# FFN gate/up of a hybrid decoder layer: 2x2 block products with seven multiplications on three of eight k-pairs

## The chip, the cores and the metric

One core of a Trainium2 chip runs one launch of the whole layer. The metric is device time in microseconds. TensorE multiplies, VectorE (DVE) and ScalarE (ACT) prepare operands and read results, SyncE (SP) issues the loads of weights; GpSimd (POOL) does next to nothing.

## The reference

The layer has 256 tokens and a width of 2048. All is float32. What the change touches is computed twice, once near the start and once near the end:

```python
def swiglu(h, wg, wu, wd):
    return (jax.nn.silu(h @ wg) * (h @ wu)) @ wd
...
x = x + 0.5 * swiglu(rmsnorm(x, g_ffn1[i]), w1_gate[i], w1_up[i], w1_down[i])
...
x = x + 0.5 * swiglu(rmsnorm(x, g_ffn2[i]), w2_gate[i], w2_up[i], w2_down[i])
```

Gate and up are 2048 x 5632 each, down is 5632 x 2048. Between the two FFNs stand latent attention, dilated window attention, their gates and projections, and after the second a gated embedding term.

## The kernel before

Every product is done in TensorE's fp32r form with operands split in two: a matrix `a` becomes `high = round(a)` and `low = a - high`, and a product is three matmuls, high x high, high x low, low x high. The activations (`hT`, 16 blocks of 128 rows of k by 256 tokens, transposed) are split once. The weights are streamed from HBM in *units* of 512 KB, 128 partitions x 1024 columns of float32, and every unit is split on its way:

- SP loads unit n into `raw[n % 4]` (`square` or `wide`; `SLOTS` = 4) once `lo_ready` says that the unit four before has been split.
- ScalarE copies it to `wh` (L741) once the DMA has landed and TensorE has finished unit n - 4 (`unit_done`).
- VectorE writes `wl = raw - wh` (L1089) and counts `lo_ready` up.
- TensorE waits for `lo_ready`, does 12 matmuls of 512 columns (2 token blocks x 2 halves of the unit x 3), and counts `unit_done` up.

In gate/up a unit is two blocks of k (a *k-pair*) by 512 columns of one matrix. A *turn* is 512 columns of gate and the same 512 of up: 16 units, first the eight k-pairs of gate into PSUM banks 0 and 1, then the eight of up into banks 4 and 5. There are 11 turns in each FFN. In the other engines' programs `ahead(u0 + j, j)` stands once per unit and splits the unit four further on, so that each engine's order is written out by hand: the splits, and between them what else is due.

At a turn's unit 7 ScalarE writes the sigmoid of the scaled gate banks into `sg` (L794) and VectorE multiplies it by the gate (L1134, `gs`); after unit 15 VectorE multiplies by up (L1140). TensorE transposes the eight 128 x 128 blocks of `gs` ahead of unit 2 of the next turn into banks 6 and 7 (`turn_blocks`, L391), and ScalarE and VectorE split them into `aTh` (L813) and `aTl` (L1158). Since the gate banks are read at unit 7 and next written a turn's half later, no unit waits for that.

Down (`down`, written out without a loop on TensorE) multiplies the 44 blocks of `aTh` and `aTl` in two halves of 1024 output columns.

`chain(...)` on VectorE lets an operation count a semaphore and has the next one wait for it: so an operation may read what the one before it wrote.

Of the kernel before, what the change touches and what calls it, by code (L numbers as in the profile page):

```python
# [48 lines left out]
def hybrid_layer(nc, out, x, p, positions, g_ffn1, w1_gate, w1_up, w1_down, g_mix, w_in, g_cq, w_uq,  # L49
# [34 lines left out]
    with ExitStack() as ctx:  # L84
# [138 lines left out]
        def _(sp):  # L223
# [58 lines left out]
            gate_up(U_GU1, w1_gate, w1_up, None)  # L282
            load_tables()
            with sp.Fori(1, FFN_TURNS) as i:
                gate_up(U_GU1, w1_gate, w1_up, i)
# [36 lines left out]
            with sp.Fori(0, FFN_TURNS) as i:  # L322
                gate_up(U_GU2, w2_gate, w2_up, i)
# [1214 lines left out]
```

## Time and profile before

| | us |
|---|---|
| median of 3 runs | 2479.52 (2479.21 to 2479.72) |
| the profiled execution | 2480.78 |
| its span | 2479.0 |
| TensorE busy | 2464.8 |
| VectorE busy | 1347.0 |
| ScalarE busy | 1150.6 |

The span runs from the first to the last instruction of the profile. A busy time is the union of an engine's instructions; matmuls overlap in their pipeline. In groups of instructions the columns are line, engine, operation, output<-input, shapes, count | busy us, mean ns of one | idle before them and what ended it. 450 MB of weights come in over the span.

### The profile page before, as it was taken

How to read it: one execution, taken by the hardware profiler on the slowest of the kernel's cores; microseconds unless marked ns; L12 is line 12 of the kernel's file. 1: busy time of each engine (PE TensorE's matmuls, PEld its weight loads, DVE VectorE, ACT ScalarE, POOL GpSimd, SP SyncE). 2: the span in 40 equal slices, each digit the busy share in tenths (PEclk: the TensorE clock that was granted, in tenths of full speed). 3: DMA queues.
4: the chain of work that ended last, by engine and by line, in shares of the span. 5: the costliest groups of instructions: out<-in, count | busy, mean ns of one | idle time of the engine just before them, and what ended most of it. 6: DMA issues, size and time to landing. Idle time of an engine off the chain costs nothing.

```text
span 2479.0 us, 31100 instructions
## 1 busy us (share of the span) xinstructions
PE 2464.8 (99%) x11314; PEld 2049.4 (83%) x11314; DVE 1347.0 (54%) x1602; ACT 1150.6 (46%) x1383; POOL 0.4 (0%) x5
## 2 busy tenths in 40 slices
PE   8999999999999999999999999999999999999999
PEld 7888888888888887888888888888888888888887
DVE  5555545554546665756655545565555555445455
ACT  5444444443435665455454444454444444434343
POOL 0000000000000000000000000000000000000000
PEclk9999999999999999999999999999999999999999
DMA  7666566655556654666644666656666666666665
GB/s 241 190 187 193 187 187 188 192 189 194 188 187 194 180 161 126 193 182 185 188 119 130 193 195 192 189 179 195 187 191 189 187 192 188 187 194 188 194 191 161
DMA packets 185635, 456.97 MB, mean 184 GB/s; under 512 B 14600, under 2 KB 15824, under 8 KB 185552
## 3 DMA queue, kind: packets, MB, share of 16 engines
q1 hardware_dynamic: 185104, 455.52, 59.9%
q8 instruction: 53, 0.87, 0.1%
q10 hardware_dynamic: 448, 0.34, 0.0%
q14 instruction: 30, 0.25, 0.0%
HBM read 453.70 MB, written 2.10 MB: 184 GB/s over the span
## 4 chain that ended last, share of the span: by engine, by line
PE 99%; DVE 0%; ACT 0%; DMA 0%; issue 0%; ACTq 0%
PE ps L361 45%; PE ps L381 16%; PE ps L383 16%; PE ps L382 16%; PE ps L471 1%; PE ps L391 1%; PE ps L487 1%; PE ps L399 1%; PE ps L498 0%; PE ps L616 0%; DMA res<-in_x 0%; DVE wl L1089 0%; ACT wh L741 0%; DVE vd L1194 0%; PE ps L550 0%; PE ps L552 0%
## 5 line engine op out<-in xcount | busy, mean ns | idle before, releaser
L1089 DVE TENSOR_TENSOR wl<-raw,wh 128x1024 fp32r<-128x1024 f32 x864 | 1056.4, 1225 | 1038.1 <-ACT wh L741 1031.0
L741 ACT ACTIVATE wh<-raw 128x1024 fp32r<-128x1024 f32 x864 | 914.5, 1060 | 1248.7 <-PE ps L383 682.6
L381 PE MATMUL ps<-wh,hT 128*128 128x512 f32 x1664 | 652.2, 392 | 2.2 <-DVE wl L1089 1.5
L383 PE MATMUL ps<-wh,hT 128*128 128x512 f32 x1664 | 648.6, 390 | 0.0
L382 PE MATMUL ps<-wl,hT 128*128 128x512 f32 x1664 | 648.5, 390 | 0.0
L361 PE MATMUL ps<-wh,hT 128*128 128x512 f32 (+1 forms) x1536 | 415.0, 388 | 1.3 <-DVE om L1221 1.1
L381 PEld LDWEIGHTS ps<-wh,hT 128*128 128x128 f32 x1664 | 313.1, 188 | 66.6 <-issue 1.9
L383 PEld LDWEIGHTS ps<-wh,hT 128*128 128x128 f32 x1664 | 312.9, 188 | 65.4
L382 PEld LDWEIGHTS ps<-wl,hT 128*128 128x128 f32 x1664 | 313.2, 188 | 63.8
L361 PEld LDWEIGHTS ps<-wh,hT 128*128 128x128 f32 x1536 | 283.6, 188 | 57.7 <-issue 1.3
L361 PE MATMUL ps<-wl,hT 128*128 128x512 f32 (+1 forms) x768 | 234.5, 387 | 0.0
L361 PE MATMUL ps<-wh,aTh 128*128 128x512 f32 x704 | 217.1, 390 | 0.0
L361 PE MATMUL ps<-wl,aTh 128*128 128x512 f32 x704 | 216.8, 389 | 0.0
L361 PE MATMUL ps<-wh,aTl 128*128 128x512 f32 x704 | 216.7, 389 | 0.0
L361 PEld LDWEIGHTS ps<-wl,hT 128*128 128x128 f32 x768 | 143.0, 188 | 29.1
L361 PEld LDWEIGHTS ps<-wl,aTh 128*128 128x128 f32 x704 | 132.1, 188 | 27.5
L361 PEld LDWEIGHTS ps<-wh,aTl 128*128 128x128 f32 x704 | 132.1, 188 | 27.4
L361 PEld LDWEIGHTS ps<-wh,aTh 128*128 128x128 f32 x704 | 131.8, 188 | 27.1
L361 PE MATMUL ps<-wh,mTh 128*128 128x512 f32 x128 | 39.6, 390 | 0.0
L361 PE MATMUL ps<-wl,mTh 128*128 128x512 f32 x128 | 39.4, 389 | 0.0
L361 PE MATMUL ps<-wh,mTl 128*128 128x512 f32 x128 | 39.4, 389 | 0.0
L1134 DVE SCALAR_TENSOR_TENSOR gs<-ps,small,sg 128x512 f32<-128x512 f32 x44 | 30.9, 743 | 1.7 <-ACT sg L794 1.7
(192 smaller groups left out, 1206.2 us busy)
## 6 DMA issues: line engine op xcount, KB each, us to landing
raw<-in_w_in SPq DMA_DIRECT2D x208, 512.0 KB, 3.6
raw<-in_w_gate SPq DMA_DIRECT2D x176, 512.0 KB, 3.5
raw<-in_w_up SPq DMA_DIRECT2D x176, 512.0 KB, 3.5
raw<-in_w_down SPq DMA_DIRECT2D x176, 512.0 KB, 3.6
raw<-in_w_o SPq DMA_DIRECT2D x32, 512.0 KB, 4.5
raw<-in_w_ple_gate SPq DMA_DIRECT2D x32, 512.0 KB, 3.6
raw<-in_w_br_mla SPq DMA_DIRECT2D x16, 512.0 KB, 4.6
raw<-in_w_br_dil SPq DMA_DIRECT2D x16, 512.0 KB, 3.6
```

The lines of the kernel that those rows point to most:

```text
L361: mm = pe.matmul(ps[:, b0 + 2 * t + m, 0:e - c], a, w[:, s, c:e], start=first, stop=last)
L381: pe.matmul(ps[:, b0 + t, :], xh, wh[:, s, c], start=first, stop=False)
L382: pe.matmul(ps[:, b0 + t, :], xh, wl[:, s, c], start=False, stop=False)
L383: mm = pe.matmul(ps[:, b0 + t, :], xl, wh[:, s, c], start=False, stop=last)
L391: mm = pe.transpose(ps[:, b0 + c // 2, c0:c0 + P], src[:, t, c * P:(c + 1) * P], ident[:, :])
L399: mm = pe.transpose(ps[:, b0 + n, s * S + t * P:s * S + (t + 1) * P], src[:, t, (2 * p + s) * P:(2 * p + s + 1) * P], ident[:, :])
L471: mm = pe.matmul(flat[:, bank * BANK + c:bank * BANK + c + keys], q, k, start=(m == 0), stop=(m == len(parts) - 1))
L487: mm = pe.matmul(ps[:, out_bank + u % 2, 0:P], values(h, t, m), pT[:, m * P:(m + 1) * P], start=(m == 0), stop=(m == n - 1))
L741: act.activation(wh[:, j % SLOTS, :], raw[:, j % SLOTS, :], ACT.Copy).then_inc(hi_ready, 1)
L1089: dve.tensor_tensor(wl[:, j % SLOTS, :], raw[:, j % SLOTS, :], wh[:, j % SLOTS, :].bitcast(F32), ALU.subtract).then_inc(lo_ready, 1)
L1134: dve.scalar_tensor_tensor(out=gs[:, t, :], in0=ps[:, t, :], scalar=inv[:, t:t + 1], in1=sg[:, t, :], op0=ALU.mult, op1=ALU.mult).then_inc ...
```

## The change

In turns 1 to 8 of the 11 of each FFN gate and up are loaded alternately, so that units 2p and 2p+1 are the k-pair p of gate (B11 over B21) and of up (B12 over B22). With the token blocks A11, A21 (first block of k) and A12, A22 (second) that is a product of 2x2 blocks, whose eight block products the k-pairs 1, 3 and 5 replace by seven of sums of blocks. A block product is three matmuls as before.

- The sums of activations (`forms`, split into `FH` and `FL`) are made once per FFN, in turn 0.
- The sums of weights (`sums`, four blocks of 512 columns) are made by VectorE (`sums_of`) once the odd unit has landed; ScalarE rounds them (`TH`), VectorE takes the rest (`TL`). `sums`, `TH` and `TL` exist once. Of the odd unit only the upper half is still split.
- A fast pair is `fast_pair`: two products out of the even unit, one out of the odd, then four with `TH` and `TL` or with a plain block of activations.
- In PSUM a fast turn uses group b0 (four banks, ends that all pairs add to) and group b1 (what the fast pairs share). The groups swap from turn to turn. VectorE combines them: `first_ends` after pair 5, `turn_ends` after unit 15. Silu and the block product then read SBUF (`ends`).
- The transposes move to pair 7. ScalarE only copies the turned blocks out (`aR`, over the place of `aTl`), since `aTh`'s place holds the new buffers; they are split in turns 9, 10 and in down.
- Sigmoid, then gate, then up becomes Silu, then up.
- SP waits for the odd unit of a fast pair before it loads into the slot of the even one.
- The loops of gate/up are written out on all engines. Turns 0, 9 and 10 keep eight products, and turn 9 and 10 wait for the Silu of the turn before at their head.

The core of the diff:

```diff
+        FH, FL = at("FH", 0, [P, 4, 3, P], F32R), at("FL", 6 * KB, [P, 4, 3, P], F32R)
+        sums, ends = at("sums", 12 * KB, [P, 4, BANK]), at("ends", 20 * KB, [P, 4, BANK])
+        TH, TL = at("TH", 28 * KB, [P, 4, BANK], F32R), at("TL", 36 * KB, [P, 4, BANK], F32R)
+        whole_x, forms = at("whole_x", 28 * KB, [P, 3, 2, S]), at("forms", 36 * KB, [P, 4, 3, P])
...
+        FAST_TURNS, FAST_PAIRS = range(1, 9), (1, 3, 5)
...
+        def free_bank(m):
+            return 0 if m % 2 else 4
...
+                        n = m * FFN_BODY + v
+                        p, w = (v // 2, (w_gate, w_up)[v % 2]) if m in FAST_TURNS else (v % 8, (w_gate, w_up)[v // 8])
+                        before = n - SLOTS
+                        square(u0 + n, v, w, 2 * p, m * BANK, 2 if before >= 0 and fast(before) and before % 2 == 0 else 1)
...
-                with pe.Fori(1, FFN_TURNS) as i:
-                    pe.wait_ge(gs_ready, PRIMED + f * T * FFN_TURNS + i * T)
...
-                        square_unit(u0 + i * FFN_BODY + j, j, 2 * j, hTh, hTl, 0, KD)
-                    for j in range(KD // 2):
-                        square_unit(u0 + i * FFN_BODY + KD // 2 + j, j, 2 * j, hTh, hTl, 4, KD)
+                for m in range(1, FFN_TURNS):
+                    if m in FAST_TURNS:
+                        fast_turn(u0, f, m)
+                    else:
+                        plain_turn(u0, f, m)
...
+            def plain_turn(u0, f, m):
+                pe.wait_ge(a_raw, f * FFN_TURNS + m - 1)
+                pe.wait_ge(sig_ready, T * (f * FFN_TURNS + m))
+                for j in range(FFN_BODY):
+                    if j == 4:
+                        pe.wait_ge(am_ready, T * (f * FFN_TURNS + m))
+                        turn_blocks(gs, 6, a_turned)
+                    square_unit(u0 + m * FFN_BODY + j, j, 2 * (j % 8), hTh, hTl, 4 * (j // 8), KD)
...
+            def fast_turn(u0, f, m):
+                u, b0, b1 = u0 + m * FFN_BODY, free_bank(m), free_bank(m + 1)
+                if m == 1:
+                    pe.wait_ge(sig_ready, T * (f * FFN_TURNS + 1))
+                else:
+                    pe.wait_ge(a_raw, f * FFN_TURNS + m - 1)
+                for p in range(KD // 2):
+                    if p == KD // 2 - 1:
+                        pe.wait_ge(am_ready, T * (f * FFN_TURNS + m))
+                        pe.wait_ge(g1_free, f * len(FAST_TURNS) + m)
+                        turn_blocks(gs, b1, a_turned)
+                    if p == FAST_PAIRS[0]:
+                        pe.wait_ge(forms_ready, f + 1)
+                        if m == 1:
+                            pe.wait_ge(am_ready, T * (f * FFN_TURNS + 1))
+                        else:
+                            pe.wait_ge(ends_ready, 2 * (f * len(FAST_TURNS) + m - 1))
+                    if p in FAST_PAIRS:
+                        fast_pair(u + 2 * p, 2 * p, p, FAST_PAIRS.index(p), b0, b1, fasts(f, m, FAST_PAIRS.index(p)))
+                    else:
+                        square_unit(u + 2 * p, 2 * p, 2 * p, hTh, hTl, b0, KD)
+                        square_unit(u + 2 * p + 1, 2 * p + 1, 2 * p, hTh, hTl, b0 + 2, KD)
+            def fast_pair(n, j, p, index, b0, b1, count):
+                s, s1, ka, kb = j % SLOTS, (j + 1) % SLOTS, 2 * p, 2 * p + 1
+                first, last = index == 0, index == len(FAST_PAIRS) - 1
+                def product(bank, x, w, start, stop):
+                    (xh, xl), (yh, yl) = x, w
+                    pe.matmul(ps[:, bank, :], xh, yh, start=start, stop=False)
+                    pe.matmul(ps[:, bank, :], xh, yl, start=False, stop=False)
+                    return pe.matmul(ps[:, bank, :], xl, yh, start=False, stop=stop)
+                def block(k, t):
+                    return hTh[:, k, t * P:(t + 1) * P], hTl[:, k, t * P:(t + 1) * P]
+                def form(a):
+                    return FH[:, a, index, :], FL[:, a, index, :]
+                def weights(slot, c):
+                    return wh[:, slot, c * BANK:(c + 1) * BANK], wl[:, slot, c * BANK:(c + 1) * BANK]
+                def summed(a):
+                    return TH[:, a, :], TL[:, a, :]
+                S1, S3, S2, S4 = (form(a) for a in range(4))
+                T1, T3, T2, T4 = (summed(a) for a in range(4))
+                pe.wait_ge(lo_ready, n + 1)
+                product(b1, block(ka, 0), weights(s, 0), first, last)
+                product(b0, block(kb, 0), weights(s, 1), False, False).then_inc(unit_done, 1)
+                pe.wait_ge(lo_ready, n + 2)
+                product(b0 + 2, S4, weights(s1, 1), False, False).then_inc(unit_done, 1)
+                pe.wait_ge(TL_ready, count + 1)
+                product(b1 + 2, S3, T3, first, last)
+                product(b1 + 3, S1, T1, first, last)
+                product(b1 + 1, S2, T2, first, last)
+                product(b0 + 1, block(kb, 1), T4, False, False).then_inc(fast_done, 1)
...
+                        if half == 0 and k == K - (12 if K == KF else 4):
                             pe.wait_ge(ready, PRIMED + after)
...
+                    target = n + SLOTS
+                    if fast(target) and target % 2:
+                        half_split(u0 + target, target)
+                        sums_high(fasts(f, target // FFN_BODY, FAST_PAIRS.index(target % FFN_BODY // 2)))
+                    else:
+                        ahead(u0 + n, n)
...
+                    if m in FAST_TURNS:
+                        if v == 2 * FAST_PAIRS[-1] + 1:
+                            act.wait_ge(fast_done, fasts(f, m + 1))
+                            act.activation(ends[:, 0, :], ps[:, free_bank(m + 1), :], ACT.Copy).then_inc(p1_out, 1)
+                        if v == FFN_BODY - 3:
+                            turned_out(f, m - 1, free_bank(m + 1))
+                        if v == FFN_BODY - 1:
+                            act.wait_ge(ends_ready, 2 * (f * len(FAST_TURNS) + m) - 1)
+                            silu(f, m, [ends[:, t, :] for t in range(T)])
+                    else:
+                        if v == KD // 2 - 1:
+                            act.wait_ge(unit_done, u0 + n + 1)
...
+                            silu(f, m, [ps[:, t, :] for t in range(T)])
+                        if m and v == 4:
+                            turned_out(f, m - 1, 6)
+                        if m and v in (5, 8, 11, 14):
+                            chunk_high(f, 4 * (m - FAST_TURNS[-1] - 1) + v // 3 - 1)
...
+            def sums_high(count):
+                act.wait_ge(sums_ready, count + 1)
+                if count:
+                    act.wait_ge(fast_done, count)
+                act.activation(TH[:, :, :], sums[:, :, :], ACT.Copy).then_inc(TH_ready, 1)
...
+            def silu(f, m, gates):
+                if f + m:
+                    act.wait_ge(am_ready, T * (f * FFN_TURNS + m))
+                for t in range(T):
+                    act.activation(sg[:, t, :], gates[t], ACT.Silu, scale=inv[:, t:t + 1]).then_inc(sig_ready, 1)
...
+            def chunk_high(f, i):
+                act.wait_ge(a_raw, f * FFN_TURNS + i + 1)
+                act.activation(aTh[:, 4 * i:4 * i + 4, :], aR[:, 4 * i:4 * i + 4, :], ACT.Copy).then_inc(ah_ready, 1)
...
+                for n in range(FFN_TURNS * FFN_BODY):
+                    m, v = divmod(n, FFN_BODY)
+                    target = n + SLOTS
+                    if m in FAST_TURNS and v == FFN_BODY - 1:
+                        turn_ends(u0 + n + 1, m)
+                    if fast(target) and target % 2:
+                        half_split(u0 + target, target)
+                        sums_rest(fasts(f, target // FFN_BODY, FAST_PAIRS.index(target % FFN_BODY // 2)))
+                    else:
+                        ahead(u0 + n, n)
+                    if fast(target) and target % 2 == 0:
+                        sums_of(u0 + target + 1, target % SLOTS,
+                                fasts(f, target // FFN_BODY, FAST_PAIRS.index(target % FFN_BODY // 2)))
+                    if v == 0 and m - 1 in FAST_TURNS:
+                        finish_block(f, m - 1, [ends[:, 2 + t, :] for t in range(T)])
+                    if m == 0:
+                        entry(2 * f, v)
+                        if 8 <= v <= 12:
+                            make_forms(f, v - 8)
+                    if m in FAST_TURNS and v == 2 * FAST_PAIRS[-1] + 1:
+                        first_ends(f, m)
+                    if m not in FAST_TURNS:
+                        if v == FFN_BODY - 1:
+                            dve.wait_ge(unit_done, u0 + n + 1)
+                            finish_block(f, m, [ps[:, 4 + t, :] for t in range(T)])
+                        if m and v in (5, 8, 11, 14):
+                            chunk_rest(f, 4 * (m - FAST_TURNS[-1] - 1) + v // 3 - 1)
+            def make_forms(f, step):
...
+                S1, S3, S2, S4 = (forms[:, a, :, :] for a in range(4))
+                if step == 0:
+                    chain(dve.tensor_tensor(whole_x[:, :, :, :], hi, lo, ALU.add))
+                if step == 1:
+                    chain(dve.tensor_tensor(S1, A21, A22, ALU.add))
+                    dve.tensor_tensor(S3, A11, A21, ALU.subtract)
+                if step == 2:
+                    chain(dve.tensor_tensor(S2, S1, A11, ALU.subtract))
+                if step == 3:
+                    dve.tensor_tensor(S4, A12, S2, ALU.subtract).then_inc(forms_raw, 1)
+                if step == 4:
+                    dve.wait_ge(forms_hi, f + 1)
+                    dve.tensor_tensor(FL[:, :, :, :], forms[:, :, :, :], FH[:, :, :, :].bitcast(F32), ALU.subtract)\
+                       .then_inc(forms_ready, 1)
...
+            def sums_of(n, s, count):
+                if count:
+                    dve.wait_ge(TL_ready, count)
+                dve.wait_ge(raw_in[s + 1], 16 * (n // SLOTS + 1))
+                B11_B12 = raw[:, s:s + 2, 0:BANK]
+                B12_B22 = raw[:, s + 1, :].rearrange("p (a c) -> p a c", a=2)
+                chain(dve.tensor_tensor(sums[:, 0:2, :], B12_B22, B11_B12, ALU.subtract))
+                chain(dve.tensor_tensor(sums[:, 2, :], raw[:, s + 1, BANK:UNIT], sums[:, 0, :], ALU.subtract))
+                dve.tensor_tensor(sums[:, 3, :], raw[:, s, BANK:UNIT], sums[:, 2, :], ALU.subtract).then_inc(sums_ready, 1)
+            def sums_rest(count):
+                dve.wait_ge(TH_ready, count + 1)
+                dve.tensor_tensor(TL[:, :, :], sums[:, :, :], TH[:, :, :].bitcast(F32), ALU.subtract).then_inc(TL_ready, 1)
+            def first_ends(f, m):
+                b1 = free_bank(m + 1)
+                dve.wait_ge(p1_out, f * len(FAST_TURNS) + m)
+                chain(dve.tensor_tensor(ends[:, 3, :], ps[:, b1 + 1, :], ends[:, 0, :], ALU.add))
+                both = ends[:, 3, :].unsqueeze(1).to_broadcast([P, 2, BANK])
+                chain(dve.tensor_tensor(ends[:, 1:3, :], ps[:, b1 + 2:b1 + 4, :], both, ALU.add))
+                dve.tensor_tensor(ends[:, 3, :], ps[:, b1 + 3, :], ends[:, 1, :], ALU.add).then_inc(g1_free, 1)
+            def turn_ends(units, m):
+                dve.wait_ge(unit_done, units)
+                b0 = free_bank(m)
+                for a in range(2):
+                    dve.tensor_tensor(ends[:, 2 * a:2 * a + 2, :], ps[:, b0 + 2 * a:b0 + 2 * a + 2, :],
+                                      ends[:, 2 * a:2 * a + 2, :], ALU.add).then_inc(ends_ready, 1)
+            def finish_block(f, m, ups):
+                if f + m:
+                    dve.wait_ge(a_turned, f * FFN_TURNS + m)
+                if m in FAST_TURNS:
+                    dve.wait_ge(ends_ready, 2 * (f * len(FAST_TURNS) + m))
+                for t in range(T):
+                    dve.wait_ge(sig_ready, T * (f * FFN_TURNS + m) + t + 1)
+                    dve.scalar_tensor_tensor(out=gs[:, t, :], in0=ups[t], scalar=inv[:, t:t + 1], in1=sg[:, t, :],
+                                             op0=ALU.mult, op1=ALU.mult).then_inc(am_ready, 1)
```

## Rows read from the trace of the kernel before

**Rows 1.** The page: TensorE's busy time, and the granted clock in 40 slices.
```profile
PE 2464.8 (99%) x11314; PEld 2049.4 (83%) x11314; DVE 1347.0 (54%) x1602; ACT 1150.6 (46%) x1383; POOL 0.4 (0%) x5
...
PEclk9999999999999999999999999999999999999999
```

**Rows 2.** The page's chain of waits, by line.
```profile
PE ps L361 45%; PE ps L381 16%; PE ps L383 16%; PE ps L382 16%; PE ps L471 1%; PE ps L391 1%; PE ps L487 1%; PE ps L399 1%; PE ps L498 0%; PE ps L616 0%; DMA res<-in_x 0%; DVE wl L1089 0%; ACT wh L741 0%; DVE vd L1194 0%; PE ps L550 0%; PE ps L552 0%
```

**Rows 3.** The chain in order of time: start, length, what; in down.
```profile
512.92 127.86 PE ps L361 x564
```

**Rows 4.** Timeline (start, length), ScalarE, the turned blocks of two turns.
```profile
114.22 1.00 ACT L813 ACTIVATE aTh<-ps 128x1024 f32 x1
...
158.63 1.01 ACT L813 ACTIVATE aTh<-ps 128x1024 f32 x1
```

**Rows 5.** Windows of one turn and of down: busy us per engine, clock, DMA.
```profile
108.40:152.80 44.40, 44.40 (x202) 36.85 (x201) 23.39 (x22) 19.05 (x19) 0.00 (x0) 1.00 0.62 189
504.00:890.00 386.00, 386.00 (x1791) 323.42 (x1790) 215.04 (x259) 196.61 (x300) 0.00 (x0) 1.00 0.60 186
```

**Rows 6.** Who waited for whom: us in total, times, longest.
```profile
DVE wl L1089 <- ACT wh L741: 1031.0, 703, 5.2
ACT wh L741 <- PE ps L383: 682.6, 437, 2.6
```

**Rows 7.** Groups of VectorE by form: split, block product, turned blocks, 512 columns.
```profile
L1089 DVE TENSOR_TENSOR wl<-raw,wh 128x1024 fp32r<-128x1024 f32 x864 | 1056.4, 1225 | 1038.1 <-ACT wh L741 1031.0
L1134 DVE SCALAR_TENSOR_TENSOR gs<-ps,small,sg 128x512 f32<-128x512 f32 x44 | 30.9, 743 | 1.7 <-ACT sg L794 1.7
L1158 DVE TENSOR_TENSOR aTl<-ps,aTh 128x1024 f32 x20 | 24.3, 1217 | 0.0
L1491 DVE TENSOR_TENSOR res<-res,sgp 128x512 f32<-128x512 f32 x4 | 2.8, 692 | 0.1
```

**Rows 8.** Timeline, all engines: a unit ends, the next begins, a slot is split.
```profile
112.83 0.39 PE L383 MATMUL ps<-wh,hT 128*128 128x512 f32 x1
113.05 0.39 PE L381 MATMUL ps<-wh,hT 128*128 128x512 f32 x1
113.25 1.06 ACT L741 ACTIVATE wh<-raw 128x1024 fp32r<-128x1024 f32 x1 [2.55 <-PE ps L383]
114.35 1.23 DVE L1089 TENSOR_TENSOR wl<-raw,wh 128x1024 fp32r<-128x1024 f32 x1 [2.38 <-ACT wh L741]
115.49 1.22 DVE L1158 TENSOR_TENSOR aTl<-ps,aTh 128x1024 f32 x1
```

**Rows 9.** Timeline, VectorE at the end: a chained operation, then an unchained one.
```profile
2471.09 0.69 DVE L1489 TENSOR_TENSOR sgp<-sgp,ps 128x512 f32<-128x512 f32 x1 [5.78 <-PE ps L361]
2471.81 0.69 DVE L1491 TENSOR_TENSOR res<-res,sgp 128x512 f32<-128x512 f32 x1
2472.42 0.68 DVE L1489 TENSOR_TENSOR sgp<-sgp,ps 128x512 f32<-128x512 f32 x1
```

**Rows 10.** Groups of ScalarE by form: split, Sigmoid, turned blocks, 512 columns.
```profile
L741 ACT ACTIVATE wh<-raw 128x1024 fp32r<-128x1024 f32 x864 | 914.5, 1060 | 1248.7 <-PE ps L383 682.6 <-PE ps L361 565.0 <-DMA raw<-in_w_gate 0.9
L794 ACT ACTIVATE sg<-ps,small 128x512 f32<-128x512 f32 x44 | 27.6, 676 | 0.0
L813 ACT ACTIVATE aTh<-ps 128x1024 f32 x20 | 20.2, 1008 | 0.0
L1069 ACT ACTIVATE pTh<-ps 128x512 fp32r<-128x512 f32 x1 | 0.6, 577 | 0.0
```

**Rows 11.** Timeline: TensorE waits for VectorE in the attention stretch.
```profile
906.86 1.28 DVE L1194 TENSOR_SCALAR vd<-ps,small 128x1024 f32<-128x1024 f32 x1
...
908.19 0.73 PE L361 MATMUL ps<-wh,hT 128*128 128x512 f32 x2 [0.20 <-DVE vd L1194]
908.76 0.62 PE L361 MATMUL ps<-wl,hT 128*128 128x512 f32 x2
```

**Rows 12.** DMA issues: count, KB each, median us to landing.
```profile
raw<-in_w_gate SPq DMA_DIRECT2D x176, 512.0 KB, 3.5
...
res<-in_x SPq DMA_DIRECT2D x4, 512.0 KB, 6.9
```

More of the change, by code:

```diff
@@ L281, in _ @@
             load_x(1)
[L282 to L285, printed above, removed]
+            gate_up(U_GU1, w1_gate, w1_up, 0)
             with sp.Fori(0, 2) as i:
@@ L449, in down @@
                             last_turn()
-                        if half == 0 and k == K - 4:
+                        if half == 0 and k == K - (12 if K == KF else 4):
                             pe.wait_ge(ready, PRIMED + after)
@@ L516, in _ @@
             gate_up(U_GU1, 0)
-            pe.wait_ge(gs_ready, PRIMED + T * FFN_TURNS)
-            down(U_DOWN1, aTh, aTl, KF, 1, a_ready, FFN_TURNS - 1, FFN_TURNS, lambda: last_a(0))
+            pe.wait_ge(sig_ready, T * FFN_TURNS)
+            down(U_DOWN1, aTh, aTl, KF, 1, a_ready, FFN_TURNS - 3, FFN_TURNS, lambda: last_a(0))
             for k in range(KD):
@@ L688, in _ @@
             gate_up(U_GU2, 1)
-            pe.wait_ge(gs_ready, PRIMED + 2 * T * FFN_TURNS)
-            down(U_DOWN2, aTh, aTl, KF, 3, a_ready, 2 * FFN_TURNS - 1, 2 * FFN_TURNS, lambda: last_a(1))
+            pe.wait_ge(sig_ready, 2 * T * FFN_TURNS)
+            down(U_DOWN2, aTh, aTl, KF, 3, a_ready, 2 * FFN_TURNS - 3, 2 * FFN_TURNS, lambda: last_a(1))
             j = 0
@@ L825, in down @@
                         ahead(u0 + half * K + k, k)
-                        if half == 0 and k == 3:
-                            last_turn()
+                        if half == 0:
+                            last_turn(k)
                         if half == 0 and meanwhile:
@@ L1154, in turned_rest, with chunk_rest, last_a @@
+            def chunk_rest(f, i):
+                dve.wait_ge(ah_ready, f * FFN_TURNS + i + 1)
+                dve.tensor_tensor(aTl[:, 4 * i:4 * i + 4, :], aR[:, 4 * i:4 * i + 4, :],
+                                  aTh[:, 4 * i:4 * i + 4, :].bitcast(F32), ALU.subtract).then_inc(a_ready, 1)
+            def last_a(f, k):
+                if k in (0, 2, 6):
+                    chunk_rest(f, (8, 9, 9, 10)[k // 2])
             def turned_rest(n, i, ready, dst, hi, done):
@@ L1175, in down @@
                         ahead(u0 + half * K + k, k)
-                        if half == 0 and k == 3:
-                            last_turn()
+                        if half == 0:
+                            last_turn(k)
                         if half == 0 and meanwhile:
@@ L1458, in _ @@
             gate_up(U_GU2, 1)
-            down(U_DOWN2, KF, 3, 0.5, lambda: last_a(1))
+            down(U_DOWN2, KF, 3, 0.5, lambda k: last_a(1, k))
             j = 0
```

145 lines of the change are left out of this document (66 added, 79 removed).

## The prediction

> **What bounds the kernel now.** The page's busy times come first: TensorE is busy 99% of 2479.0 us, with the granted clock at its upper level (2.4 GHz) in every slice, and no clock is to be won back [rows 1]. The chain of waits agrees: it is matmuls almost to the end [rows 2]. In order of time it has 564 matmuls in one unbroken run of 127.86 us, so one matmul costs 0.2267 us; the 390 ns of the groups is the length of one in a pipeline, not its spacing [rows 3]. A unit of weights (512 KB, 12 matmuls) is 2.72 us. In gate/up a turn starts 44.41 us after the last, read from one copy of turned blocks to the next [rows 4]; 192 matmuls make 43.53, eight transposes the other 0.88, and nothing is idle. So each matmul removed is worth its full 0.227 us, as long as VectorE and ScalarE still deliver. They have room now: VectorE is busy 23.4 us of 44.4 [rows 5], and mostly waits for ScalarE, which waits for TensorE to free a slot [rows 6].
>
> **Removed.** A fast pair has seven products of three matmuls (21) instead of 24. 3 pairs x 8 turns x 2 FFNs x 3 = 144 matmuls x 0.2267 = **-32.65 us**. A fast turn is ideally 183 matmuls and 8 transposes, 42.37 us, a gain of 2.04. The same bytes are loaded.
>
> **Prices.** VectorE: 1024 columns 1.225 us, 512 columns 0.69, a scaled product of 512 columns 0.74 [rows 7]; the slope is 1.04 ns per column, so 2048 columns are 2.29 (from the nearest rows: two passes of 1024 give 2.28 as spacing and 2.37 as length). Where the next operation waits for nothing it starts 0.085 us before the last one's end (1.14 us after a 1024 pass), where it waits for ScalarE 0.04 us after ScalarE's end; ScalarE starts 0.20 us after the next unit's first matmul [rows 8]. An operation chained to the one before starts 0.03 us after its end: 0.72 us apart for 512 columns, 0.61 unchained [rows 9]. ScalarE: 1024 columns 1.06, 512 from PSUM 0.58 against 1.01 for 1024, so 512 from SBUF 0.63 and 2048 1.92 (two passes bound it at 2.03) [rows 10]. TensorE starts 0.05 us after VectorE's end and loses 0.1 on the first two matmuls [rows 11].
>
> **Added on VectorE, per fast turn.** 13 full splits at 1.14 (14.8), 3 half splits at 0.60 (1.8), 3 times sums (1.26 + 0.72 + 0.69, 8.0), 3 residuals of 2048 columns at 2.21 (6.6), first ends 2.6, turn ends 2.3, the two block products 1.3: 37.4 us of 42.4. That would fit. But the queue is in order, and behind each sums_of it has only a half split to do while ScalarE makes TH (0.04 + 1.92 + 0.04): 1.4 us idle three times, 41.6 in all. And slots set how far it may run ahead. So I follow the queue. Y is when TensorE starts unit 15, the last of a turn; units are loaded into four slots, and unit n+4 is split once unit n is done.
>
> *To the first fast pair of the next turn.* ScalarE copies slot 2 from Y+0.20 to 1.26; VectorE splits from 1.30, sums from 2.44 to 5.10, two turn ends to 7.38, half split, residual from 7.90 to 10.21. Unit 15, for which the turn ends wait, is done by Y+2.92. TensorE, at its own pace, starts pair 1 at Y+8.16 and needs the residual after nine matmuls, at 10.20: late by 0.06 with the 0.05 of handing over. The wait for the turn ends (7.38) doesn't bind.
>
> *To pair 3.* Let t=0 be the start of pair 1. The residual ended at t=2.05. Now come the split of slot 4 (1.14), the block products (1.32), splits 5 and 6 (2.28), sums (2.66, to 9.38), TH to 11.34, residual to **13.69**. TensorE needs it at 4.76 + 5.44 + 2.04 = 12.24, or 12.30 after the first delay: **a stall of 1.44**. What is queued behind the residual, the splits of slots 8 and 9, isn't late: pair 3's own last 12 matmuls cover it.
>
> *To pair 5.* Splits 8, 9, 10, sums, TH and residual take 10.3 against 10.2 of matmuls: 0.1 late, more or less swallowed by the two restarts. After that there are four plain units and pairs 6 and 7: first ends are through 1.1 us before the transposes need bank group b1, and VectorE is idle again at Y. The lateness doesn't grow from turn to turn.
>
> A turn so loses 1.6 to 1.7 of its 2.04. I take 1.65. This holds for turns 2 to 8: 14 x 1.65 = **+23.1**.
>
> *Turn 1* has no ends before it, but the block products of turn 0 stand behind the residual: 9.41, then to 10.73; pair 1 waits for them, 10.78 - 8.16 + 0.1 = 2.7. VectorE then starts the turn level and is not late at pair 3 (residual at 10.8 of 12.24). Two such: **+5.4**.
>
> *Turn 9* (plain) waits at its head for the silu of turn 8, which needs the first turn end: unit 15 done + 0.20, VectorE 1.22, ScalarE 0.04, two silus 0.58 + 0.73 (Sigmoid's 0.68 and 0.05 for SBUF [rows 10]; Silu isn't in the trace, a copy's 0.63 and 1.06 for 1024 columns bound it), 0.1: 2.9. Before, the gate banks had eight units of cover. Two: **+5.8**.
>
> **At nothing.** The forms (two passes of 1536 columns, four of 384, about 5.7 us per FFN) lie in turn 0, where VectorE idles 1.5 us in each of eight units; uncovered they would cost those 5.7. The aTh/aTl splits, now out of SBUF, move to turns 9, 10 and down: 2.1 us beside 2.72 of matmuls; one more copy of 1.0 goes on ScalarE, which then has 23 us of 42 (13 splits 12.6, half splits 1.6, TH 5.5, the rest 3). Silu takes the place of Sigmoid and of its one table load per FFN. Down waits for all blocks at k=32, the last is there by k=8. Unrolled code runs gapless in down [rows 3]; the loops cost nothing either, so no gain. DMAs: a slot's next load after an even fast unit is held until the odd one's half split; both then go out together. SP is past everything else at that time.
>
> Sum: -32.65 + 23.1 + 5.4 + 5.8 = **+1.7** against the profiled execution, 2480.8, which is 1.3 above the median shown. So 2479.5 + 1.7 = **2481**.
>
> **A rule against a row.** Unchained and chained operations of 512 columns are 0.61 and 0.72 us apart [rows 9]. The Trainium skill, VectorE: DVE Perf Modes, section "The DRAIN you can't avoid", has it that the semaphore after an operation costs nothing extra. The trace disagrees by 0.11.
>
> **Rivals.** *(a) VectorE keeps up, faster.* If the stalls before the residuals vanish, -32.65 + 5.4 + 5.8 = -21.5: 2458. Half of them, 2470. For it: 37.4 of 42.4 us busy, and each saving of 0.1 us per step over the ten steps to pair 3 is 1 us. Against: each step has a row.
>
> *(b) Chaining is free.* Each sums_of is 0.22 shorter: the first residual is in time, pair 3 waits 1.05, pair 5 nothing; 0.6 less per turn, 14 x 0.6 + 0.4 = 8.8 off: 2472. This is what the Trainium skill's rule named above would give; rows 9 speak against it.
>
> *(c) The odd slot comes late, slower.* Slots 6 and 7 are both requested when the half split of slot 3 ends, t=-0.2. In my sum they are there by 3.4 and 5.5: 3.5 us for one load, and the other behind it; VectorE wants slot 6 split by 5.57, and ScalarE has that by 4.5. Loads of x that went out beside others took 6.9 [rows 12]. Then slot 7 lands at 7.2, 0.5 after sums_of wants it (6.71), the same at pair 5 (17.4 for 17.0): 0.9 more per turn, 14 x 0.9 = 12.6: 2494. It decides from 6.9 us after release on. For: 1 MB at once; against: DMA is 62% busy [rows 5].
>
> *(d) It doesn't do what it says:* the matmuls stay at 11314 and the waits come on top, 2514.
>
> **Chances.** Forecast (2475 to 2487) 0.40; (a) 0.25; (b) 0.07; (c) 0.24; (d) and the like 0.04. Under about 0.2%, 5 us, this kernel's measurement can't tell a difference. Faster: (a) and half of (b), 0.29. Same: 0.33 of the forecast, the rest of (b), 0.02 of (c): 0.38. Slower: 0.33. Range 2461 to 2499: 0.25 us of stall per turn is 3.5 us, so it holds stalls from 0.2 to 2.9 per turn.
>
> **What would show it.** Matmuls 11170. Turns 2 to 8 at 44.0 us instead of 44.41, each with one TensorE idle of some 1.4 us behind VectorE's 2048-column residual, at pair 3; at pairs 1 and 5 under 0.2. Turn 1 an idle of 2.6 behind the block product, turn 9 one of 2.8 behind the silu. VectorE busy some 88% in fast turns. Wrong would be: VectorE waiting for loads (c), no idle at pair 3 (a), idle before pairs 1 and 5 as long as before 3 (steps priced too low).

## The result, and the profile after

| | before | changed |
|---|---|---|
| median, 7 runs each on the same chips, us | 2479.52 (2478.07 to 2480.11) | 2486.32 (2484.95 to 2489.76) |
| ratio | | 1.0031, 95% interval 1.0021 to 1.0041 |
| profiled execution, its span | 2480.78, 2479.0 | 2484.95, 2483.2 |
| mean granted clock of TensorE in the 7 runs | | 0.997 to 0.999 |

The changed kernel is 0.3% slower, 6.8 us. The forecast was 2481, the range 2461 to 2499. The execution with the profile was the fastest of the seven; its span is 4.2 us above that of before, and not 6.8, for a reason that lies in the first microseconds of both (last section).

The page of the changed kernel, busy times, then the chain of waits by engine and by line, then the groups of the new operations on VectorE and ScalarE:

```profile
PE 2440.8 (98%) x11170; PEld 2018.1 (81%) x11170; DVE 1589.3 (64%) x1842; ACT 1244.3 (50%) x1470; POOL 0.4 (0%) x5
...
PE 86%; DVE 9%; ACT 2%; issue 2%; DMA 1%; SPq 0%; ACTq 0%
PE ps L382 45%; PE ps L402 10%; PE ps L404 10%; PE ps L403 10%; PE ps L502 2%; DVE TL L1329 2%; PE ps L503 2%; PE ps L504 2%; DVE wl L1222 2%; DVE sums L1323 1%; DVE ends L1344 1%; ACT TH L923 1%; PE ps L561 1%; PE ps L412 1%; PE ps L577 1%
...
L923 ACT ACTIVATE TH<-sums 128x2048 fp32r<-128x2048 f32 x48 | 92.1, 1919 | 147.3 <-DVE sums L1325 147.3
...
L1329 DVE TENSOR_TENSOR TL<-sums,TH 128x2048 fp32r<-128x2048 f32 x48 | 109.9, 2290 | 47.0 <-ACT TH L923 47.0
...
L1323 DVE TENSOR_TENSOR sums<-raw 128x1024 f32<-128x1024 f32 x48 | 58.5, 1218 | 0.0
```

11170 matmuls are 144 fewer than in [rows 1]. The two operations of 2048 columns, of which the kernel before had none, take 2.29 and 1.92 us, as the slope had it. Most telling is the chain of waits: in [rows 2] it is matmuls, here 9% of it is VectorE.

One turn in a window (its ends and length, then busy us of PE, PEld, DVE, ACT, POOL, then the granted clock as a share of 2.4 GHz, the DMA share and GB/s). It runs from the first turn end on VectorE to the next one. It answers to [rows 5]:

```profile
148.57:192.63 44.06, 42.97 (x193) 34.95 (x192) 37.20 (x36) 23.50 (x23) 0.00 (x0) 1.00 0.60 191
```

44.06 instead of 44.41. VectorE is busy 37.2 us instead of 23.4. TensorE's matmuls and transposes would fill 42.37, so 1.69 are lost. Where, the timeline of VectorE says (start, length), from the ends of one turn to pair 3 of the next; the last row is TensorE's:

```profile
148.57 2.35 DVE L1344 TENSOR_TENSOR ends<-ps,ends 128x1024 f32<-128x1024 f32 x2
...
150.84 0.68 DVE L1313 TENSOR_TENSOR wl<-raw,wh 128x512 fp32r<-128x512 f32 x1
151.44 2.29 DVE L1329 TENSOR_TENSOR TL<-sums,TH 128x2048 fp32r<-128x2048 f32 x1
153.64 1.22 DVE L1222 TENSOR_TENSOR wl<-raw,wh 128x1024 fp32r<-128x1024 f32 x1
154.78 1.41 DVE L1354 SCALAR_TENSOR_TENSOR gs<-ends,small,sg 128x512 f32<-128x512 f32 x2
156.10 2.35 DVE L1222 TENSOR_TENSOR wl<-raw,wh 128x1024 fp32r<-128x1024 f32 x2
158.37 1.22 DVE L1323 TENSOR_TENSOR sums<-raw 128x1024 f32<-128x1024 f32 x1
159.62 0.69 DVE L1324 TENSOR_TENSOR sums<-raw,sums 128x512 f32<-128x512 f32 x1
160.35 0.69 DVE L1325 TENSOR_TENSOR sums<-raw,sums 128x512 f32<-128x512 f32 x1
160.96 0.69 DVE L1313 TENSOR_TENSOR wl<-raw,wh 128x512 fp32r<-128x512 f32 x1
163.03 2.29 DVE L1329 TENSOR_TENSOR TL<-sums,TH 128x2048 fp32r<-128x2048 f32 x1 [1.38 <-ACT TH L923]
165.38 0.50 PE L502 MATMUL ps<-TH,FH 128*128 128x512 f32 x1 [1.09 <-DVE TL L1329]
```

Read it as a queue without a gap from 148.57 to 161.6: ends, half split, residual, three splits with the block products between them, sums. Then 1.38 us in which VectorE has nothing to do but wait for TH, then the residual, and TensorE starts 0.06 after it. The residuals end 11.59 us apart (153.73 and 165.32); the matmuls between their uses take 10.2. Measured from start to start of the matmuls of this turn, 1.39 of the 1.69 are lost at pair 3 (1.26 before the first matmul with TH, 0.13 over the next ones), 0.23 at pair 1 and 0.07 at pair 5.

Whom TensorE waited for over the whole execution (us in total, times, longest):

```profile
PE ps L502 <- DVE TL L1329: 15.3, 14, 1.1
...
PE ps L402 <- issue: 5.5, 2, 2.7
PE ps L502 <- issue: 5.1, 2, 2.5
PE ps L382 <- issue: 1.9, 2, 0.9
```

Fourteen times pair 3; twice the head of turn 9 (L402); twice pair 1 of turn 1 (L502); and twice the head of down (L382), which the prediction had left out. The times are from a matmul's modelled end, 0.16 us behind where the next would have started. "Issue" is here a wait whose releaser the profile doesn't show. The timeline has the block products of turn 0 end at 64.96 and the silu of turn 8 at 413.40, each just before the matmul that waited:

```profile
61.35 2.29 DVE L1329 TENSOR_TENSOR TL<-sums,TH 128x2048 fp32r<-128x2048 f32 x1 [1.38 <-ACT TH L923]
63.56 1.40 DVE L1354 SCALAR_TENSOR_TENSOR gs<-ps,small,sg 128x512 f32<-128x512 f32 x2
65.06 0.47 PE L502 MATMUL ps<-wh,hT 128*128 128x512 f32 x1 [2.54 <-issue]
...
410.81 2.36 DVE L1344 TENSOR_TENSOR ends<-ps,ends 128x1024 f32<-128x1024 f32 x2 [0.34 <-PE ps L404]
412.07 1.33 ACT L929 ACTIVATE sg<-ends,small 128x512 f32<-128x512 f32 x2
413.51 0.47 PE L402 MATMUL ps<-wh,hT 128*128 128x512 f32 x1 [2.73 <-issue]
```

The granted clock around turn 1 of the second FFN (windows, columns as above; the clock is the third number from the end), then TensorE there:

```profile
1692.00:1694.00 2.00, 0.65 (x3) 0.19 (x2) 2.00 (x2) 1.45 (x2) 0.00 (x0) 1.00 1.01 380
1694.00:1696.00 2.00, 0.81 (x2) 0.74 (x3) 2.00 (x3) 0.00 (x0) 0.00 (x0) 0.79 0.25 97
1696.00:1698.00 2.00, 2.00 (x6) 1.52 (x6) 1.36 (x2) 0.00 (x0) 0.00 (x0) 0.50 0.35 39
1698.00:1700.00 2.00, 2.00 (x9) 1.64 (x8) 0.72 (x1) 1.61 (x2) 0.00 (x0) 0.86 0.98 341
```

```profile
1695.19 0.76 PE L502 MATMUL ps<-wh,hT 128*128 128x512 f32 x1 [2.54 <-issue]
1695.75 0.63 PE L503 MATMUL ps<-wl,hT 128*128 128x512 f32 x1
1696.18 0.63 PE L504 MATMUL ps<-wh,hT 128*128 128x512 f32 x1
1696.61 0.63 PE L502 MATMUL ps<-wh,hT 128*128 128x512 f32 x1
```

After 2.54 us without a matmul the clock is found to have fallen to 1.2 GHz for 3.4 us in all; matmuls then start 0.43 us apart instead of 0.227, and the stretch costs about 1.7 us. The same idle in the first FFN, 2.54 us as well, has no such stretch in this execution.

### The profile page after: what moved, and what is told of

The parts are those of the page before. It is cut to its first block, busy times and chain, and to the rows that moved or that the text cites. A ratio compares the mean times of both kernels' runs of the same rounds, so it can differ in the third digit from the quotient of the medians.

```text
span 2483.2 us, 29387 instructions
## 1 busy us (share of the span) xinstructions
PE 2440.8 (98%) x11170; PEld 2018.1 (81%) x11170; DVE 1589.3 (64%) x1842; ACT 1244.3 (50%) x1470; POOL 0.4 (0%) x5
## 3 DMA queue, kind: packets, MB, share of 16 engines
q8 instruction: 80, 1.31, 0.2%
## 4 chain that ended last, share of the span: by engine, by line
PE 86%; DVE 9%; ACT 2%; issue 2%; DMA 1%; SPq 0%; ACTq 0%
PE ps L382 45%; PE ps L402 10%; PE ps L404 10%; PE ps L403 10%; PE ps L502 2%; DVE TL L1329 2%; PE ps L503 2%; PE ps L504 2%; DVE wl L1222 2%; DVE sums L1323 1%; DVE ends L1344 1%; ACT TH L923 1%; PE ps L561 1%; PE ps L412 1%; PE ps L577 1%
## 5 line engine op out<-in xcount | busy, mean ns | idle before, releaser
L1222 DVE TENSOR_TENSOR wl<-raw,wh 128x1024 fp32r<-128x1024 f32 x816 | 988.3, 1223 | 748.4 <-ACT wh L831 745.8
L831 ACT ACTIVATE wh<-raw 128x1024 fp32r<-128x1024 f32 x816 | 857.7, 1058 | 969.1 <-PE ps L382 564.8
L402 PE MATMUL ps<-wh,hT 128*128 128x512 f32 x1280 | 501.7, 392 | 7.9 <-issue 5.5
L404 PE MATMUL ps<-wh,hT 128*128 128x512 f32 x1280 | 498.3, 389 | 0.0
L403 PE MATMUL ps<-wl,hT 128*128 128x512 f32 x1280 | 498.1, 389 | 0.0
L382 PE MATMUL ps<-wh,hT 128*128 128x512 f32 (+1 forms) x1536 | 415.0, 388 | 1.2 <-DVE om L1431 1.0
L382 PEld LDWEIGHTS ps<-wh,hT 128*128 128x128 f32 x1536 | 283.5, 188 | 57.5 <-issue 1.2
L402 PEld LDWEIGHTS ps<-wh,hT 128*128 128x128 f32 x1280 | 240.4, 188 | 57.6 <-issue 8.2
L404 PEld LDWEIGHTS ps<-wh,hT 128*128 128x128 f32 x1280 | 240.3, 188 | 50.1
L403 PEld LDWEIGHTS ps<-wl,hT 128*128 128x128 f32 x1280 | 240.5, 188 | 48.6
L382 PE MATMUL ps<-wl,hT 128*128 128x512 f32 (+1 forms) x768 | 234.5, 387 | 0.0
L382 PE MATMUL ps<-wh,aTh 128*128 128x512 f32 x704 | 217.3, 390 | 1.9 <-issue 1.9
L382 PE MATMUL ps<-wh,aTl 128*128 128x512 f32 x704 | 216.8, 389 | 0.0
L382 PE MATMUL ps<-wl,aTh 128*128 128x512 f32 x704 | 216.7, 389 | 0.0
L382 PEld LDWEIGHTS ps<-wl,hT 128*128 128x128 f32 x768 | 143.0, 188 | 29.1
L923 ACT ACTIVATE TH<-sums 128x2048 fp32r<-128x2048 f32 x48 | 92.1, 1919 | 147.3 <-DVE sums L1325 147.3
L382 PEld LDWEIGHTS ps<-wh,aTh 128*128 128x128 f32 x704 | 131.7, 188 | 29.7 <-issue 2.6
L382 PEld LDWEIGHTS ps<-wh,aTl 128*128 128x128 f32 x704 | 132.2, 188 | 27.5
L382 PEld LDWEIGHTS ps<-wl,aTh 128*128 128x128 f32 x704 | 132.2, 188 | 27.4
L1329 DVE TENSOR_TENSOR TL<-sums,TH 128x2048 fp32r<-128x2048 f32 x48 | 109.9, 2290 | 47.0 <-ACT TH L923 47.0
L502 PE MATMUL ps<-TH,FH 128*128 128x512 f32 x144 | 60.0, 416 | 15.3 <-DVE TL L1329 15.3
L1323 DVE TENSOR_TENSOR sums<-raw 128x1024 f32<-128x1024 f32 x48 | 58.5, 1218 | 0.0
```

Source lines behind the costliest of these rows:

```text
L382: mm = pe.matmul(ps[:, b0 + 2 * t + m, 0:e - c], a, w[:, s, c:e], start=first, stop=last)
L402: pe.matmul(ps[:, b0 + t, :], xh, wh[:, s, c], start=first, stop=False)
L403: pe.matmul(ps[:, b0 + t, :], xh, wl[:, s, c], start=False, stop=False)
L404: mm = pe.matmul(ps[:, b0 + t, :], xl, wh[:, s, c], start=False, stop=last)
L502: pe.matmul(ps[:, bank, :], xh, yh, start=start, stop=False)
L831: act.activation(wh[:, j % SLOTS, :], raw[:, j % SLOTS, :], ACT.Copy).then_inc(hi_ready, 1)
```

## The experiments

All are made from the changed kernel, but the last. Each was timed beside the kernel before on the same chip. For gap, gap_early, turn0 and heads that kernel took 2479.51 there, as beside the changed kernel (2479.52). For moved, all4 and idle20, on another chip, it took 2477.90: their distance to the changed kernel is therefore taken from their distances to the kernel before, each on its own chip.

**gap.** In turns 2 to 8 the block products fill the wait for TH.

```diff
                         half_split(u0 + target, target)
+                        if v == 3 and m - 1 in FAST_TURNS:
+                            finish_block(f, m - 1, [ends[:, 2 + t, :] for t in range(T)])
                         sums_rest(...)
...
-                    if v == 0 and m - 1 in FAST_TURNS:
+                    if v == 0 and m - 1 == FAST_TURNS[-1]:
```

> The block products of turn m-1 move from behind the split of slot 4 to behind the half split of pair 3, where VectorE idles 1.38 us for TH. Order theory: they leave the leg to pair 3 (1.32 us). But slot 6 is then the limit: ScalarE had it split 4.8 us into pair 1 in the changed kernel, so VectorE splits at 4.8 and not at 4.25, and the stall at pair 3 goes from 1.44 to about 0.6: turns 2 to 8 at 43.3 instead of 44.06, 14 x 0.8 = 11 us faster, 2475. Were only VectorE's steps in the way: stall 0.1, 18 us, 2468. Load theory (slots 6 and 7 decide): VectorE only idles more, stall 1.2 or more, under 3 us faster.

Measured: 2475.32 (2472.93 to 2480.85, 11 runs), ratio to the kernel before 0.9985 [0.9976, 0.9994]: 11.0 us under the changed kernel. VectorE in the same leg:

```profile
156.99 2.35 DVE L1222 TENSOR_TENSOR wl<-raw,wh 128x1024 fp32r<-128x1024 f32 x2
159.57 1.23 DVE L1222 TENSOR_TENSOR wl<-raw,wh 128x1024 fp32r<-128x1024 f32 x1 [0.23 <-ACT wh L831]
...
163.91 1.41 DVE L1356 SCALAR_TENSOR_TENSOR gs<-ends,small,sg 128x512 f32<-128x512 f32 x2
165.38 2.29 DVE L1331 TENSOR_TENSOR TL<-sums,TH 128x2048 fp32r<-128x2048 f32 x1
```

and ScalarE, whose split of slot 6 waited for the load:

```profile
158.47 1.06 ACT L831 ACTIVATE wh<-raw 128x1024 fp32r<-128x1024 f32 x1 [1.39 <-DMA raw<-in_w_gate]
```

The products now stand where nothing else could, and the residual starts the moment TH is there (ScalarE ends it at 165.34). The third split waits for ScalarE and that for the load. The load was not what held the changed kernel, but it is next in line. The turns of the first FFN take 42.87 to 43.47 us, on average 43.13 (43.3 was expected): 14 x 0.94 = 13 us less. The medians show 11.0; the profiled execution has one stretch at the lower clock more than that of the changed kernel.

**gap_early.** The same, and slots 6 and 7 are let go earlier.

```diff
                         half_split(u0 + target, target)
+                        if m in FAST_TURNS and v == FFN_BODY - 1:
+                            turn_ends(u0 + n + 1, m)
...
-                    if m in FAST_TURNS and v == FFN_BODY - 1:
+                    if m == FAST_TURNS[-1] and v == FFN_BODY - 1:
                         turn_ends(u0 + n + 1, m)
...
```

> As gap, and the half split of slot 3 goes ahead of the two turn ends, so that the loads of slots 6 and 7 are let go 2.3 us earlier. Turn ends are then through 0.2 us before pair 1 wants them. Order theory with the load as second limit: stall at pair 3 0.1 to 0.2, turns at 42.8, 14 x 1.25 = 17.5 us faster than the changed kernel, 2469, and 6 us faster than gap. If the load is no limit: the same as gap.

Measured: 2469.32 (2467.76 to 2472.09, 5 runs), 0.9958 [0.9945, 0.9972], 6.0 under gap. VectorE does the three splits in one piece:

```profile
153.72 3.49 DVE L1222 TENSOR_TENSOR wl<-raw,wh 128x1024 fp32r<-128x1024 f32 x3
```

and TensorE's waits for TL are no longer among its own; only its weight loads show them, 0.3 at most:

```profile
PEld ps L502 <- DVE TL L1333: 9.1, 42, 0.3
```

**moved.** The counter-test: the same 1.32 us out of one leg and into the next.

```diff
-                    if v == 0 and m - 1 in FAST_TURNS:
+                    if v == (5 if m in FAST_TURNS else 0) and m - 1 in FAST_TURNS:
                         finish_block(...)
```

> The block products of turn m-1 move, in turns 2 to 8, from behind the split of slot 4 to behind the split of slot 9, out of the leg to pair 3 and into the leg to pair 5. Order theory: the stall isn't removed but goes where the 1.32 us go. Pair 3 waits 0.3 to 0.6 (slot 6's load, as in gap), pair 5 waits about 1.2: turns as in the changed kernel or up to 0.3 longer, 2486 to 2490. Rival (VectorE has too much to do over the whole turn, or one long wait at pair 3 has a cause of its own): pair 5 waits no longer than in gap, 2475.

Measured: 2496.45 (2493.45 to 2501.35, 4 runs), 1.0072 [1.0056, 1.0089]. The stall did move; in the turn at 150 us TensorE waits 0.32 at pair 3 and 1.09 at pair 5:

```profile
169.43 0.50 PE L502 MATMUL ps<-TH,FH 128*128 128x512 f32 x1 [0.32 <-DVE TL L1329]
181.02 0.50 PE L502 MATMUL ps<-TH,FH 128*128 128x512 f32 x1 [1.09 <-DVE TL L1329]
```

The total was priced too low, by 6 us and more. The turn is 44.60 (sums start at 150.81 and 195.41), 0.54 more than in the changed kernel instead of up to 0.3: 14 x 0.54 = 7.6. By the starts of its matmuls pair 5 now loses the whole 1.39 that pair 3 lost before, and pair 3 still loses 0.62, since the third split waits 0.46 for ScalarE and that for the load, as in gap. To the kernel before beside it there are 18.6 us, and from the changed kernel to its own 6.8: 11.8 between the two. The 4.2 that the turns leave over fit in part with three stretches at the lower clock in the profiled execution against one, but that is one execution of each.

**turn0.** The block products of turn 0 go ahead of the residual.

```diff
                         half_split(u0 + target, target)
+                        if m == 0:
+                            dve.wait_ge(unit_done, u0 + n + 1)
+                            finish_block(f, m, [ps[:, 4 + t, :] for t in range(T)])
                         sums_rest(...)
...
-                        if v == FFN_BODY - 1:
+                        if v == FFN_BODY - 1 and m:
                             dve.wait_ge(unit_done, u0 + n + 1)
                             finish_block(f, m, [ps[:, 4 + t, :] for t in range(T)])
```

> Only the block products of turn 0 go ahead of the residual, into the wait for TH. Order theory: the idle of 2.54 us at pair 1 of turn 1 is gone, 2 x 2.7 = 5.4 us. Clock theory (TensorE's clock falls to its lower level around such an idle in some executions, 1.7 us each time): on top of that about 1 us less, and the granted clock is higher. 2480 to 2481. Rival: the residual itself is late for pair 1 (it ends 0.8 before it is wanted by my sum), then 2.0 of the 2.7 stay.

Measured: 2480.85 (2479.18 to 2485.02, 11 runs), 1.0009 [1.0, 1.0018]: 5.5 less. The 5.1 us of idle before L502 are gone from TensorE's waits. The second half of the expectation failed: the granted clock is no higher than in the changed kernel (0.997 to 0.999). Its mean was 0.998 in nine of the eleven runs and 1.0 in two, which took 2479.18 and 2479.31, against 2480.51 to 2485.02 in the nine. The profiled execution has a stretch at the lower clock behind one of the two idles of turn 9 and another at 11.8 us, at the first matmuls.

**heads.** Two waits that guard nothing where they stand.

```diff
 def plain_turn(u0, f, m):
-                pe.wait_ge(sig_ready, T * (f * FFN_TURNS + m))
+                if m > FAST_TURNS[-1] + 1:
+                    pe.wait_ge(sig_ready, T * (f * FFN_TURNS + m))
...
-                        if half == 0 and k == K - (12 if K == KF else 4):
+                        if half == 0 and k == K - (20 if K == KF else 4):
...
-            down(U_DOWN1, aTh, aTl, KF, 1, a_ready, FFN_TURNS - 3, FFN_TURNS, ...)
+            down(U_DOWN1, aTh, aTl, KF, 1, a_ready, FFN_TURNS - 4, FFN_TURNS, ...)
...
```

> Two waits that guard nothing at that place: turn 9's head no longer waits for the silu of turn 8 (its banks 0 and 1 were read before the transposes of turn 8), and down starts with 7 of 11 blocks of turned products, and waits for the rest at k=24 instead of 32. Expected: 2 x 2.9 at turn 9 and 2 x 1.1 at the head of down, 8.0 us: 2478. If the clock falls around the idle of turn 9 in some executions, 1 us more. Rival: silu and turn ends run into the next use of their banks, and TensorE waits at k-pair 4 of turn 9 instead: under 3 us.

Measured: 2477.88 (2476.29 to 2480.77, 11 runs), 0.9995 [0.9986, 1.0004]: 8.4 less. The idles at L402 and L382 that had "issue" as their end are gone from TensorE's waits. In the changed kernel the head of down looks like this: VectorE does the eighth block behind the split of a slot, TensorE waits for it:

```profile
501.08 1.23 DVE L1222 TENSOR_TENSOR wl<-raw,wh 128x1024 fp32r<-128x1024 f32 x1 [1.49 <-ACT wh L831]
502.23 1.22 DVE L1359 TENSOR_TENSOR aTl<-aR,aTh 128x1024 fp32r<-128x1024 f32 x1
...
503.55 0.70 PE L382 MATMUL ps<-wh,aTh 128*128 128x512 f32 x2 [0.93 <-issue]
```

**all4.** gap_early, turn0 and heads in one kernel.

```diff
                         half_split(u0 + target, target)
+                        if m in FAST_TURNS and v == FFN_BODY - 1:
+                            turn_ends(u0 + n + 1, m)
+                        if m == 0:
+                            dve.wait_ge(unit_done, u0 + n + 1)
+                            finish_block(f, m, [ps[:, 4 + t, :] for t in range(T)])
+                        if v == 3 and m - 1 in FAST_TURNS:
+                            finish_block(f, m - 1, [ends[:, 2 + t, :] for t in range(T)])
                         sums_rest(...)
...
```

> gap_early, turn0 and heads in one. If the causes are separate they add up: 2469.3 (gap_early) - 5.4 (turn 1) - 8.0 (turn 9, head of down) = 2456. Clock theory: no TensorE idle over 1 us is left in gate/up, so no stretch at the lower level in gate/up and 1 to 3 us on top: 2453 to 2455. The ideal, 144 matmuls less and nothing else, would be 2446.9. If one stall comes back in the next turn: 2460 or more.

Measured: 2451.35 (2450.26 to 2453.10, 4 runs), ratio to the kernel before 0.9893 [0.9876, 0.9909]. A turn, from turn ends to turn ends:

```profile
144.88:187.61 42.73, 42.73 (x193) 34.86 (x192) 37.18 (x37) 23.28 (x24) 0.00 (x0) 1.00 0.62 197
```

42.73 with the same 37.2 us of VectorE, so it was the order and not the amount. What is left over the ideal 42.37, 0.36 a turn, stands where TensorE takes up new sums (0.24 at pair 1, 0.07 at pair 3, 0.05 at pair 5). Against the changed kernel: 14 x 1.33 = 18.6, 5.4, 5.8 and 2.2 are 32.0. By the distances to the kernel before, 26.6 under it here and 6.8 over it there, 33.4 were won; the raw medians are 35.0 apart, but 1.6 of that is the other chip. Some 1.4 us are left for the clock, which was 1.0 in every run. The two profiled executions, matched matmul by matmul, fit with that: 34.5 us apart at the last one, of which 1.6 is the one stretch at the lower clock. So the clock gave 1 to 2 us, within the 1 to 3 expected; the median lies under the 2453 expected by as much as the chip is faster.

**idle20.** The kernel before, with a long idle at the head of 20 turns.

```diff
                     pe.wait_ge(gs_ready, PRIMED + f * T * FFN_TURNS + i * T)
+                    pe.wait_ge(am_ready, PRIMED + f * T * FFN_TURNS + i * T)
```

> The kernel before, with one wait more at the head of each of the 20 turns after the first ones: TensorE waits there for the second block product of the turn before. Nothing is left out. By VectorE's and ScalarE's rows each idle is 3.8 to 4.0 us: 20 x 3.9 = 78, 2557. Clock theory: the clock falls to its lower level behind a part of the idles, 3.4 us at half speed each time, 1.7 us lost: if one in three, 11 us more, 2568, and the mean granted clock about 0.995. No-clock theory: 2557, clock as in the kernel before.

Measured: 2615.22 (2612.48 to 2616.45, 4 runs), 1.055 [1.0532, 1.0568], clock 0.974 to 0.975. Two of the windows at the end of one idle, where the clock is 0.53 and 0.50:

```profile
60.00:62.00 2.00, 1.03 (x3) 0.85 (x4) 0.73 (x2) 0.00 (x0) 0.00 (x0) 0.53 0.63 157
62.00:64.00 2.00, 2.00 (x6) 1.63 (x5) 0.00 (x0) 0.00 (x0) 0.00 (x0) 0.50 0.31 120
```

and whom TensorE waited for:

```profile
PE ps L381 <- DVE gs L1141: 79.7, 20, 4.3
```

The idles are what they were priced at, 79.7 us. The rest of the 137 is a lower clock, and the expectation had its share far too small: at every one of the 20 idles the clock fell, for 6.8 us, not for 3.4 behind one in three. It fell 0.9 to 1.4 us before the idle ended, so that some 5.5 us of each stretch held matmuls, 0.43 us apart: 20 x 5.5 / 2 = 55 us.

## Why the prediction was right, point by point

- **Matmuls removed, -32.65.** Right: 144 fewer, 0.227 us apart where nothing waits and the clock is not low.
- **Turns 2 to 8, +23.1.** Right: 1.69 lost per turn for 1.65, 14 x 1.69 = 23.7, and 1.39 of the 1.69 at the place named, pair 3 (1.44 was worked out). The residuals stand 11.59 us apart for the 11.64 worked out. gap took the block products out of that leg, moved put them into the next one, and the stall followed both times. VectorE is busy 84% of such a turn (37.20 of 44.06), not the 88% given as a sign: that was its 37.4 over the ideal 42.4.
- **Turn 1, +5.4.** Right: TensorE starts pair 1 at 65.06 us, where 62.36 was due (the last matmul before began at 62.13), 2.70 late; turn0 gave back 5.5.
- **Turn 9, +5.8.** Right: 2.89 for 2.9, from the same reckoning (413.51 for 410.62).
- **"Down waits for all blocks at k=32, the last is there by k=8", at nothing.** This is the term that failed. The other wait of down, at its head, wants eight blocks, and the eighth is split behind unit 14 of turn 10. 1.1 us each (503.55 for 502.45), 2.2 in both. The diff has it, and it wasn't followed.
- **"No clock is to be won back".** True, but the sum took for granted that none is lost. The change makes four idles of 2.5 to 2.7 us, and behind some of them TensorE runs at 1.2 GHz for 3.4 us; the profiled execution has one such stretch. all4, with no such idle, has none and won 1.4 us more than the stalls removed, about one stretch per execution; idle20 shows the effect by itself, though with longer idles.
- **Sum.** In the first FFN turn 1 begins at 56.92 us and down at 503.55, 446.63 us, where the kernel before has 59.59 and 503.72, 444.13: 2.5 us more, with no stretch at the lower clock between them. By the terms it is -16.3 + 11.8 + 2.7 + 2.9 + 1.1 = 2.2. Twice 2.5 and one stretch at the lower clock (1.7) are 6.7 of the 6.8 between the medians; how many stretches the other executions had is not on record. Single spans aren't to be compared to a microsecond: the two profiled ones are 4.2 apart, because the kernel before there began turn 1 2.7 us later, with its first matmuls 0.43 us apart. Of the 5.3 us between 2481 and 2486.3, 2.2 are down's, 0.6 the turns', 1.7 the clock's, and 0.8 are not assigned. All lie on one side, and no error of any size hid another. The time came out on the slower side of the 0.2%, for which 0.33 was given.
- **Rivals.** (a) VectorE did not keep up in this order; gap_early is the kernel that (a) described. It took 2469.3 and not 2458, though (a) had turns 1 and 9 in its sum: 0.36 a turn stay (5.0 us), 2.2 are down's, and two stretches at the lower clock in its profiled execution are 3.4. (b) The trace decides for the rows: the sums start at 158.37, 159.62 and 160.35, 1.25 and 0.73 apart where chained, and the half split at 160.96, 0.61 later unchained. (c) The odd slot did not hold up anything in the changed kernel: VectorE never waited for a load ahead of sums. Slot 7 had landed 5.0 us behind the start of pair 1, and the sums that read it began at 6.7. gap showed a late load for slot 6, as the second limit; letting it go earlier was worth 6.0 us. (d) fell with the count.

## What to carry to other kernels

When matmuls are traded for work on another engine, its busy share (37 us of 42) doesn't tell whether it keeps up. Follow its queue from one use of its result to the next, with each wait for another engine in it, and compare that with what TensorE does in between. Then look for work that can stand inside such a wait: moving two operations into one was worth 11 us, and all the edits of all4 together 33. An idle of TensorE of some 2.5 us can cost more than its length, for the clock may fall behind it.

## What the runs showed of the hardware

- Idles of 2.5 to 2.7 us were followed by 3.4 us at 1.2 GHz in 11 of 20 cases in six profiled executions: one of four in the changed kernel, two of four in gap and in gap_early, three of four in moved, one of the two left in turn0 (at turn 9) and both of the two left in heads (at turn 1). The longer ones were not followed by it more often: 8 of 10 at turn 1 (2.54 us), 3 of 10 at turn 9 (2.73 us). The stretch began between 0.6 us before the idle's end and 1.4 us behind it. What decides between the cases was not tried.
- Idles of 4.0 us (idle20) had 6.8 us of it 20 times of 20, beginning 0.9 to 1.4 us before the idle's end. Idles of 1.1 us at pair 3 had none.
- In six of the nine profiled executions, that of the kernel before among them, the first matmuls at 11 us are 0.43 us apart for 3 to 6 us; in those of the changed kernel, all4 and idle20 they are not. In five of the six the row of the granted clock shows nothing of it. Two matmuls and a window of the kernel before:

```profile
12.04 0.63 PE L383 MATMUL ps<-wh,hT 128*128 128x512 f32 x1
12.47 0.63 PE L381 MATMUL ps<-wh,hT 128*128 128x512 f32 x1
...
12.00:14.00 2.00, 2.00 (x6) 1.56 (x5) 2.00 (x4) 1.80 (x4) 0.00 (x0) 1.00 1.05 392
```

- all4, with the stalls of all four places removed, ran at a clock of 1.0 in every run and varies by 2.8 us over four; gap varies by 7.9 over eleven, with clocks of 0.996 to 0.999.
- The instruction queues carry 1.31 and 0.34 MB instead of 0.87 and 0.25 for the loops written out; of TensorE's idles above 0.8 us inside the two FFNs none goes back to it.
